# Sliding-window attention: the softmax division moved from the probabilities to the attention outputs

## The reference, cut to what matters

```python
sc = jnp.einsum('bqhgd,bkhd->bhgqk', qb, kbb) * scale      # 64 ** -0.5
sc = jnp.where(mb, sc, NEG_INF)
m = jnp.maximum(jnp.max(sc, axis=-1, keepdims=True), sink)
p = jnp.exp(sc - m)
p = p / (jnp.sum(p, axis=-1, keepdims=True) + jnp.exp(sink - m))
return jnp.einsum('bhgqk,bkhd->bqhgd', p, vbb)
...
return o @ w_o
```

## Time and profile before

| | |
|---|---|
| median of 3 runs | 1338.01 us (1337.99 to 1338.21) |
| profiled execution, its own time | 1337.57 us |
| profiled execution, span from first to last instruction | 1335.4 us |
| TensorE busy | 1299.5 us, 97% of the span |
| VectorE busy | 890.3 us, 67% |
| ScalarE busy | 352.4 us, 26% |
| mean granted TensorE clock | 0.994 |

### The profile page before, as it was taken

One profiled execution on the slowest core, in us unless ns is written; L12 is line 12 of the kernel. 1 busy time (PEld: TensorE's weight loads), 2 busy tenths in 40 slices (PEclk: granted clock), 3 DMA queues, 4 the chain that ended last, 5 costly groups with the idle time before them and its releaser, 6 DMA issues.

```text
span 1335.4 us, 25145 instructions
## 1 busy us (share of the span) xinstructions
PE 1299.5 (97%) x10828; PEld 994.6 (74%) x10828; DVE 890.3 (67%) x1504; ACT 352.4 (26%) x756; POOL 119.9 (9%) x184
## 2 busy tenths in 40 slices
PE   7999999999999999899999999998899999999999
PEld 6868648689996444569999457866788776999943
DVE  4588663567787346738989749376665474798973
ACT  2311210312221023612333013612433441233300
POOL 4746000000000011000000000021100000000000
PEclk9989999999999999899999999999999999999999
DMA  8533342345445534044454462510010053445452
GB/s 306 184 126 127 126 147 106 126 151 187 141 179 190 188 126 159 31 158 149 167 190 152 173 241 68 193 55 3 3 35 14 24 190 126 135 182 188 140 185 87
DMA packets 16734, 182.31 MB, mean 137 GB/s; under 512 B 1648, under 2 KB 3952, under 8 KB 6000
## 3 DMA queue, kind: packets, MB, share of 16 engines
q1 hardware_dynamic: 14320, 175.12, 36.0%
q10 hardware_dynamic: 2304, 5.59, 1.1%
HBM read 179.65 MB, written 1.05 MB: 135 GB/s over the span
## 4 chain that ended last, share of the span: by engine, by line
PE 93%; DVE 4%; ACT 1%; issue 1%; DMA 0%; POOL 0%; DVEq 0%; POOLq 0%
PE banks L1763 28%; PE banks L1780 15%; PE banks L1473 11%; PE banks L1440 11%; PE banks L1450 4%; PE banks L2078 3%; PE banks L2067 2%; PE banks L1728 2%; PE banks L1657 2%; PE banks L1426 2%; PE banks L2085 1%; PE banks L2223 1%; PE banks L1922 1%; DVE weight_ring L3243 1%; PE banks L1910 1%
## 5 line engine op out<-in xcount | busy, mean ns | idle before, releaser
L1763 PE MATMUL banks<-xn,arena 128*128 128x128 f32 x1440 | 165.7, 275 | 0.0
L1763 PEld LDWEIGHTS banks<-xn,arena 128*128 128x128 f32 x1440 | 163.2, 192 | 0.0
L1780 PE MATMUL banks<-arena 128*128 128x512 f32 x264 | 121.9, 592 | 0.0
L1763 PE MATMUL banks<-hT,weight_ring 128*128 128x128 f32 x960 | 116.5, 275 | 0.0
L1763 PEld LDWEIGHTS banks<-hT,weight_ring 128*128 128x128 f32 x960 | 111.8, 192 | 0.0
L1473 PE MATMUL banks<-weight_ring,arena 128*128 128x512 f32 x224 | 97.7, 593 | 0.8 <-ACT arena L1364 0.8
L1780 PEld LDWEIGHTS banks<-arena 128*128 128x128 f32 x264 | 49.8, 190 | 60.7 <-issue 60.7
L1780 PE MATMUL banks<-weight_ring,arena 128*128 128x512 f32 x198 | 93.3, 592 | 0.0
L2836 DVE SCALAR_TENSOR_TENSOR arena<-arena,prm 128x255 f32<-128x255 f32 x200 | 87.4, 479 | 5.4 <-ACT arena L1104 3.6
L1473 PEld LDWEIGHTS banks<-weight_ring,arena 128*128 128x128 f32 x224 | 42.2, 190 | 51.3 <-issue 49.7
L1104 ACT ACTIVATE arena<-arena,prm 128x256 f32<-128x256 f32 x100 | 54.7, 593 | 86.3 <-issue 44.2
(11 more groups left out here) (455 smaller groups left out, 2153.4 us busy)
## 6 DMA issues: line engine op xcount, KB each, us to landing
weight_ring<-in_wall SPq DMA_DIRECT2D x81, 2048.0 KB, 8.1
weight_ring<-in_wall SPq DMA_DIRECT2D x2, 1024.0 KB, 7.3
x<-in_x_tok ACTq DMA_DIRECT2D x2, 512.0 KB, 4.6
arena<-in_mem_tok SPq DMA_DIRECT2D x1, 1024.0 KB, 17.7
arena<-in_wall SPq DMA_DIRECT2D x1, 1024.0 KB, 5.5
arena<-in_wide SPq DMA_DIRECT2D x2, 512.0 KB, 4.2
out_y<-x ACTq DMA_DIRECT2D x4, 256.0 KB, 2.0
arena<-in_masks ACTq DMA_DIRECT2D x1, 896.0 KB, 9.6
```

Source lines behind the costliest of these rows:

```text
L1763: ins = mm(b_(n)[:, j * P:(j + 1) * P], lhsT=weights[:, kb, j * P:(j + 1) * P], rhs=features_[:, kb, :], start=opens and j == 0 and kb == ...
L1780: ins = mm(b_(n), lhsT=a, rhs=b, start=pair == 0, stop=pair == FB // 2 - 1)
```

## The change

The probabilities are no longer scaled. TensorE transposes them as soon as the exponentials are read out, and the multiplication by the values is done the other way round: a 128x128 block of `w_pT` is the stationary operand, and the moving one is 65 columns of a new tile `w_v`, which are a head's 64 value features and a column of ones. So the row sum comes out as column 65. VectorE adds the sink, takes the reciprocal and multiplies the 128x256 output by it into `w_o`; TensorE turns that with two transposes, and the result is copied to `w_oT` by VectorE (ScalarE for the last two units). The copies of the values' projection go to `w_v` (one more ScalarE instruction for a token tile). The values are multiplied once for every unit, one unit later than their transposes. The diff, cut to its core:

```diff
     for u in range(8):
-        out += [(f"sw_s{u + 2}", 1, f"pair{u % 2}")] * (u < 6) + [(f"sw_t{u}", 1, "pair2")] + [("q_tr_b", 2, 6, 7)] * (u == 1)
-        out += [(f"sw_ov{u // 2 - 1}", 1, 6)] * (u > 0 and u % 2 == 0)
-    out += [("sw_ov3", 1, 6)]
+        out += [(f"sw_s{u + 2}", 1, f"pair{u % 2}")] * (u < 6) + [(f"sw_ot{u - 2}", 1, 6)] * (u > 1)
+        out += [(f"sw_t{u}", 1, "pair2")] + [("q_tr_b", 2, 6, 7)] * (u == 1) + [(f"sw_ov{u - 1}", 1, 6)] * (u > 0)
+    out += [("sw_ov7", 1, 2), ("sw_ot6", 1, 6), ("sw_ot7", 1, 3)]
...
# ScalarE
                         ins = A(w_p[...], pair_(n)[...], ACT.Exp,
-                                scale=1 / 8, bias=nb[:, at:at + 1], accum_out=den[:, at:at + 1])
+                                scale=1 / 8, bias=nb[:, at:at + 1])
...
-            def window_out(q):
+            def window_out(u):
...
-                if u and u % 2 == 0:
-                    window_out(u // 2 - 1)
-            window_out(3)
+            for u in (6, 7):
+                window_out(u)
...
# TensorE
             def window_columns(u):
-                pe.wait_ge(sw_p, u + 1)
+                pe.wait_ge(*when_read(G[f"sw_s{u}"]))
...
-            def window_values(q):
...
+            def window_values(u):
+                n = G[f"sw_ov{u}"]
+                free(n)
+                pe.wait_ge(*when_read(G[f"sw_t{u}"]))
+                for tt in range(TT):
+                    for i in range(2):
+                        for m in range(TT):
+                            ins = mm(b_(n)[:, (2 * tt + i) * (HD + 1):][:, :HD + 1],
+                                     lhsT=w_pT[:, (u % 4) * 1024 + i * 512 + m * T + tt * P:][:, :P],
+                                     rhs=w_v[:, m, 2 * (u // 4) + i, :], start=m == 0, stop=m == TT - 1)
+                ins.then_inc(psum_full, 1)
+
+            def turn_values(u):
+                n = G[f"sw_ot{u}"]
+                pe.wait_ge(*when_read(G[f"sw_ov{u}"]))
+                free(n)
+                for tt in range(TT):
+                    ins = nc.tensor.transpose(b_(n)[:, tt * P:(tt + 1) * P], w_o[:, u % 2, tt * P:(tt + 1) * P], ident)
+                ins.then_inc(psum_full, 1)
...
             for u in range(8):
                 if u < 6:
                     window_scores(u + 2)
+                if u > 1:
+                    turn_values(u - 2)
                 if u in (4, 6):
                     swa_out(0, range(u - 4, u - 2))
...
-                if u and u % 2 == 0:
-                    window_values(u // 2 - 1)
+                if u:
+                    window_values(u - 1)
             for c in range(2):
-                swa_out(c, range(4, 6))
-            window_values(3)
+                swa_out(c, range(4, 5))
+            swa_out(0, range(5, 6))
+            window_values(7)
+            turn_values(6)
+            swa_out(1, range(5, 6))
+            swa_out(0, range(6, 7))
+            turn_values(7)
+            swa_out(1, range(6, 7))
             for c in range(2):
-                swa_out(c, range(6, KB))
+                swa_out(c, range(7, KB))
...
# VectorE
-            def window_p(u):
-                dve.wait_ge(sw_exp, u + 1)
-                do(tt_(den[:, at], den[:, at], dsk[:, at], ALU.add))
-                do(V.reciprocal(den[:, at], den[:, at]))
-                for m in range(4):
-                    part = w_p[:, (u % 4) * 1024 + m * T:][:, :T]
-                    ins = ts_(part, part, den[:, 4 * u + m:4 * u + m + 1], None, ALU.mult)
-                ins.then_inc(sw_p, 1)
+            def window_scaled(u):
+                n = G[f"sw_ov{u}"]
+                sums = b_(n, 4 * (HD + 1)).rearrange("p (m c) -> p m c", m=4)
+                dve.wait_ge(sw_exp, u + 1)
+                dve.wait_ge(psum_full, n + 1)
...
+                do(tt_(total..., sums[:, :, HD]..., by_tile(dsk), ALU.add))
+                do(V.reciprocal(total, total))
+                tt_(h64b(w_o[:, u % 2, :]), sums[:, :, 0:HD], spread(total, HD), ALU.mult).then_inc(bank_sem(n), 1)
+
+            def window_out(u):
+                n = G[f"sw_ot{u}"]
+                dve.wait_ge(psum_full, n + 1)
+                V.tensor_copy(w_oT[:, u, :], b_(n, T)).then_inc(bank_sem(n), 1)
+
+            step(V.memset(w_v[:, :, :, HD:HD + 1], 1.0))
             for u in range(2):
+                window_mask(u)
                 window_max(u)
             for u in range(8):
-                window_p(u)
                 if u == 0:
                     last_sums(1)
                 if u == 1:
                     last_norms(1)
+                if u < 6:
+                    window_mask(u + 2)
+                if u > 1:
+                    window_out(u - 2)
                 if u < 6:
                     window_max(u + 2)
...
+                if u:
+                    window_scaled(u - 1)
+            window_scaled(7)
```

More of the change, by code:

```diff
@@ L646, in build @@
         head_root = sem("head_root")
-        sw_p = sem("sw_p")
         x_mixed = sem("x_mixed")
@@ L750, in build @@
         qkv = qkv.rearrange("p (t d) -> p t d", t=TT)
+        w_v, w_o = carve(25088, TT * 4 * (HD + 1), 2 * 2 * P)
+        w_v = w_v.rearrange("p (t h c) -> p t h c", t=TT, h=4)
+        w_o = w_o.rearrange("p (b n) -> p b n", b=2)
         w_sq = w_sq.rearrange("p (t d) -> p t d", t=TT)
@@ L1173, in qkv_out @@
                 if c == 0:
-                    A(qkv[:, tt, :].rearrange("p (m n) -> p m n", n=256)[:, 0:6:5, :], b3(n, 2, 256), ACT.Copy)
+                    A(qkv[:, tt, 0:256], b_(n, 256), ACT.Copy)
+                    A(w_v[:, tt, :, 0:HD], b_(n)[:, 256:512].rearrange("p (h c) -> p h c", h=4), ACT.Copy)
                     A(w_sq[:, tt, 0:256], b_(n, 256), ACT.Square).then_inc(bank_sem(n), 1)
@@ L1205, in window_columns @@
                 A(w_pT[:, (u % 4) * 1024:][:, :1024].rearrange("p (b n) -> p b n", b=2), pair_(n), ACT.Copy).then_inc(bank_sem(n), 1)
-            def window_out(q):
-                n = G[f"sw_ov{q}"]
+            def window_out(u):
+                n = G[f"sw_ot{u}"]
                 act.wait_ge(psum_full, n + 1)
-                A(w_oT[:, 2 * q:2 * q + 2, :], b3(n, 2, T), ACT.Copy).then_inc(bank_sem(n), 1)
+                A(w_oT[:, u, :], b_(n, T), ACT.Copy).then_inc(bank_sem(n), 1)
             window_exp(0)
@@ L1920, in swa_out @@
                 for kb in blocks:
-                    pe.wait_ge(*when_read(G[f"sw_ov{kb // 2}"]))
+                    pe.wait_ge(*when_read(G[f"sw_ot{kb}"]))
                     ins = mm(b_(n), lhsT=w_oT[:, kb, 0:P], rhs=wc[:, kb * 512:(kb + 1) * 512],
@@ L3039, in _, with window_mask @@
             last_norms(0)
-            def window_max(u):
+            def window_mask(u):
                 n = G[f"sw_s{u}"]
@@ L3045, in window_max @@
                 band = pair_(n)[:, :, P:P + T]
+                do(tt_(band, band, tiled(swc[:, P:P + T], 2), ALU.min))
+            def window_max(u):
+                n = G[f"sw_s{u}"]
                 at = slice(4 * u, 4 * u + 4)
-                do(tt_(band, band, tiled(swc[:, P:P + T], 2), ALU.min))
                 do(V.tensor_reduce(mx[:, at], halves_(n), AX, ALU.max))
@@ L3050, in window_max @@
                 tt_(dsk[:, at], nb[:, at], sink_neg[:, at], ALU.subtract).then_inc(sw_max, 1)
-            def window_p(u):
-                at = slice(4 * u, 4 * u + 4)
+            def window_scaled(u):
+                n = G[f"sw_ov{u}"]
+                sums = b_(n, 4 * (HD + 1)).rearrange("p (m c) -> p m c", m=4)
                 dve.wait_ge(sw_exp, u + 1)
-                do(tt_(den[:, at], den[:, at], dsk[:, at], ALU.add))
-                do(V.reciprocal(den[:, at], den[:, at]))
-                for m in range(4):
-                    part = w_p[:, (u % 4) * 1024 + m * T:][:, :T]
-                    ins = ts_(part, part, den[:, 4 * u + m:4 * u + m + 1], None, ALU.mult)
-                ins.then_inc(sw_p, 1)
+                dve.wait_ge(psum_full, n + 1)
+                by_tile = lambda ap: ap[:, 4 * u:4 * u + 4].rearrange("p (i t) -> p t i", i=2)
+                total = den[:, 4 * u:4 * u + 4]
+                do(tt_(total.rearrange("p (t i) -> p t i", t=2), sums[:, :, HD].rearrange("p (t i) -> p t i", t=2), by_tile(dsk), ALU.add))
+                do(V.reciprocal(total, total))
+                tt_(h64b(w_o[:, u % 2, :]), sums[:, :, 0:HD], spread(total, HD), ALU.mult).then_inc(bank_sem(n), 1)
+            def window_out(u):
+                n = G[f"sw_ot{u}"]
+                dve.wait_ge(psum_full, n + 1)
+                V.tensor_copy(w_oT[:, u, :], b_(n, T)).then_inc(bank_sem(n), 1)
+            step(V.memset(w_v[:, :, :, HD:HD + 1], 1.0))
             for u in range(2):
+                window_mask(u)
                 window_max(u)
             for u in range(8):
-                window_p(u)
                 if u == 0:
```

## The result

The changed kernel has a median of 1347.76 us (4 runs, 1345.94 to 1347.79) against 1338.0 for the kernel before (4 runs, 1337.08 to 1338.21), a ratio of 1.0074 with a 95% interval of 1.0062 to 1.0086. The forecast was 1346.1 us with a range of 1342.5 to 1350.0. The profiled execution took 1347.76 us, span 1345.9.

What follows compares the result with a forecast made beforehand. VectorE bounds the attention up to 542.4 us, TensorE afterwards. Values +7.0, turning +2.1, scores 4 +1.1, waits +1.7, clock +0.1, front -3.5 and averages -0.3 make 8.1 us later: 1346.1 us, range 1342.5 to 1350.0.

Steps and rivals of the forecast that it cites:

- What bounds the kernel: Attention of tile 0: VectorE sets the half up to 542.4 us, TensorE, 32.81 of 33.60 us busy, the rest.
- The front half, -3.5: Up to the values of unit 0: without scalings in VectorE's order they start at 538.9 in place of 542.4 us.
- The values, +7.0: Value products on TensorE: 128 rows in place of 64, load sets 0.115 us a row, 14.7 us in all.
- The turning, +2.1: New turning of the outputs on TensorE: 16 transposes at 0.128 us each, 2.05 us.
- The waits, +1.7: Turning waits 1.09 us for VectorE in steps 6 and 7; with small waits 2.5, less the present 0.8.
- The small waits: Second half, TensorE: waits of 0.1 us for bank 6 or for the scaling, 0.3 us together.
- The clock, +0.1: One clock fall after the thin front stretch, met by the values of unit 0: 1.84 us more, against 1.7 before.
- All of it reaches the end: Behind the stretch the order is as before, so the 8.1 us delay reaches the end whole.
- Rival A: Value products: moving width sets the step, 0.064 us a row; +1.3 us, 1339.3; chance 0.06.
- rival B: Value products: stationary loads hidden altogether, TensorE never waits for VectorE; 3.9 us earlier, 1334.1; chance 0.04.
- Rival C: Steps 6 and 7, thin margins in 2 and 3: clock falls twice more after waits, +3.4 us, 1349.5; chance 0.13.
- D: Front half: clock stays up as transposes no longer wait, -1.8 us, 1344.3; lower edge of the forecast's 0.77.

Runs made afterwards that it cites:

- The later turning: Changed kernel with the turning of units 4 and 5's outputs behind the projection's pieces of steps 6 and 7: stretch 52.77 us against 55.17, ratio 1.0051.
- The fill: Changed kernel with 22 spare identity transposes in TensorE's idle time ahead of the values of unit 0: stretch 52.26 us, 2.91 less, ratio 1.0038.

## Why the prediction was right, step by step

- **What bounds the kernel.** Right. Taking the scaling away alone gives 2.65 us, but for a small share of the clock all in the front, and the accumulator reads give nothing (55.18 against 55.17).
- **The front half, -3.5.** Right: 538.70 against 538.9 for the start of the values.
- **The values, +7.0.** Right in size and reason: at full clock the groups take 1.73 to 1.96 us a unit, on average 1.8 (1.84 forecast), which is 0.3 us less in all; half of the products make 6.7 us, and 128 columns in place of 65 only 0.4. But the sentence that the load sets the step held only for whole loads; that it could be got round by halves at the same cost in columns was not in the prediction.
- **The turning, +2.1.** Right together with the transposes behind it. The chain of the changed kernel reads:

```profile
549.04 0.41 PE banks L1922 x2
549.45 0.87 PE banks L1900 x8
```

The two make 1.28 us, and I had 0.26 + 1.02 = 1.28. Taken alone, the pairs are 0.8 us more than forecast (0.41 in six of eight steps, the low clock taken out, and 0.22 in two) and the six groups of transposes 0.9 less; the chain only puts the border elsewhere.
- **The waits, +1.7.** Right to 0.1: 1.09 us twice. The later turning took both away, for 2.40 us. The old wait of 0.8 ahead of the projection's end is gone, as forecast. The small waits, 0.3 in the forecast, are 0.1 in the chain.
- **The clock, +0.1.** This term was mis-sized. I counted one low time of 3.4 us that meets the values of unit 0. It lasted 6.8 and met scores 4, the first turning and transposes 2 as well: 1.7 + 0.95 + 0.2 + 0.5, about 3.4 us where I had 1.8. These 1.6 and the turning's 0.8, less 0.9 on the transposes, 0.3 on the values, 0.2 on the small waits and 0.2 in front, leave 0.8 of the 0.9 us by which the stretch was longer than the forecast 8.1. The fill gave 2.91 of the 3.4 back. So the forecast came close by its sum, and its one term that was clearly off is the clock's.
- **All of it reaches the end.** Right: 8.9 us at 946 us of the span. The further 1.6 of the profiled execution arise in an unchanged phase in which the clock was low; they lie within that phase's spread, and the forecast had nothing for it.

Rival A is refuted by the profile (0.112 us from row to row) and by the wider operand, rival B with it. Beside rival A the prediction set figures by moving columns from the Trainium skill, "TensorE: Matmul & The Clock Gate", section "Back-to-back issue gap", and said that the trace contradicts them. That section gives them for a matmul by itself and says that in a stream of loads and matmuls both set the spacing, with which these rows agree in so far as the load does it here: 0.112 us at 65 columns as at 128. Rival C expected the clock to fall again behind the waits of steps 6 and 7. It did not: the granted clock is 1.00 from 546 us to the end of the stretch. What came was one low time in front, twice as long, 1.6 us more and half of C's 3.4. D, a clock that stays up in the front, came in the changed kernel only where spare transposes were added.

What stays open: why the same low time lasts 3.4 us in one run of the changed work and 6.8 in another. Fills or shorter gaps went with no fall in the stretch in five of the kernels, but what decides its length no run here isolates, and each kernel has only one execution with a trace.

## What to carry to other kernels

Before turning a product round so that its long side becomes the stationary operand, count the stationary loads, not the multiplications: here 64 rows became 128 at nearly the same price each, 7 us against 2.65 to win. Where such products can't be avoided, cut the stationary operand into two column halves and issue them in alternation; here that took about 5.5 us off. Work that is taken from an engine is worth something only in the part of the time in which that engine's order decides; here two evictions moved to ScalarE gave 1.3 us there, about half of what all the scaling had to give. With the clock, which stayed up in that execution, it was 3.0.

## What the hardware showed that I had not expected

- Twice the number of float32 matmul rows took 60% of the time: 128x128 by 65 columns 1.73 to 1.96 us a unit, the same in alternating 64-column halves 1.08, in halves one after the other 1.83. Each half keeps its 0.058 us from row to row while the other works between.
- Spare transposes keep the clock up: with 22 of them in idle time of about 3 us the granted clock stayed at 1.00, for 2.9 us less in the stretch.
- A low clock can come in a phase far from the change: the same instructions, with 0, 3.4 or 6.8 us of low clock among them, took 197.9 to 201.5 us.
